# State space heads of one block: channels on partitions, heads in pairs, a channel mean by a matmul

## What is computed

```python
a_cum = jnp.cumsum(dt * A, axis=-1)
lmat = jnp.exp(segsum(a))
y_diag = jnp.einsum('bgcls,bgrcls,bcsgrp->bclgrp', cb, lmat, xc)
y_off = jnp.einsum('bclgn,bcgrpn,bgrcl->bclgrp', cc, prev_states, jnp.exp(a_cum))
y = y_f + flip(y_b) + d_skip[:, :, None] * xs
gated = y.reshape(bsz, length, g, r * p) * jax.nn.silu(zs)
gated = gated * lax.rsqrt(jnp.mean(gated * gated, axis=-1, keepdims=True) + EPS)
out = gated.reshape(bsz, length, D_SSD) * norm_w
```

## Time and profile before

| | us |
|---|---|
| median of 3 runs | 2029.85 (2029.8 to 2035.62) |
| profiled execution | 2027.07 |
| its span | 2025.3 |
| TensorE busy | 1749.7 (86%) |
| VectorE busy | 639.7 (32%) |
| ScalarE busy | 320.4 (16%) |
| GpSimd busy | 99.8 (5%) |
| transfers, mean over the span | 266 GB/s |

### The profile page before, as it was taken

How to read it: one execution, slowest core, us unless ns; L and a number is a source line. 1 busy time by engine, 2 the same in 40 slices (tenths; PEclk the granted TensorE clock), 3 DMA queues, 4 the chain that set the end, 5 groups by cost and what they waited for, 6 DMA issues and landing times.

```text
span 2025.3 us, 23132 instructions
## 1 busy us (share of the span) xinstructions
PE 1749.7 (86%) x9670; PEld 869.3 (43%) x9670; DVE 639.7 (32%) x1486; ACT 320.4 (16%) x715; POOL 99.8 (5%) x95
## 2 busy tenths in 40 slices
PE   6999999889999998989999989889998856665655
PEld 3844544444444476433333323246474423332322
DVE  2157828751310285231321312131353101010101
ACT  2112222210301265010000000020341000000000
POOL 0000112250200000000000000000000000000000
PEclk9899999889999999999999999999999978788877
DMA  8241238674612202179999999951308999999996
GB/s 331 104 167 58 109 125 319 262 287 175 241 42 83 83 1 98 55 299 427 428 428 428 427 427 427 427 211 52 140 1 332 377 427 427 427 427 427 427 427 267
DMA packets 39099, 538.20 MB, mean 266 GB/s; under 512 B 4330, under 2 KB 4714, under 8 KB 6612
## 3 DMA queue, kind: packets, MB, share of 16 engines
q1 hardware_dynamic: 37860, 530.85, 63.4%
q0 software_dynamic: 1136, 5.88, 0.8%
HBM read 535.66 MB, written 1.05 MB: 265 GB/s over the span
## 4 chain that ended last, share of the span: by engine, by line
PE 52%; issue 29%; DMA 10%; DVE 4%; POOL 2%; ACT 1%; DVEq 1%; POOLq 1%; SPq 0%; ACTq 0%
PE bank L596 51%; DMA mem<-in_moe 8%; PE bank L606 2%; DMA mem<-in_w_ada 1%; DVE mem L1306 1%; DVEq L1303 1%; POOL mem L2284 0%; POOLq L2285 0%; POOL mem L2296 0%; POOL mem L2287 0%; DMA mem<-in_ada_w 0%; POOL mem L2278 0%; POOL mem L2245 0%; DVE mem L1768 0%; ACT mem L1977 0%
## 5 line engine op out<-in xcount | busy, mean ns | idle before, releaser
L596 PE MATMUL bank<-mem 128*32 128x256 f32 (+10 forms) x8934 | 1642.7, 499 | 251.6 <-DMA mem<-in_moe 163.0
L596 PEld LDWEIGHTS bank<-mem 128*32 128x32 f32 (+5 forms) x8934 | 786.2, 151 | 1063.5 <-issue 753.7
L1977 ACT ACTIVATE mem<-bank 128x512 f32<-128x512 f32 (+5 forms) x279 | 141.5, 513 | 1165.6 <-PE bank L596 839.6
L1768 DVE TENSOR_TENSOR mem<-mem,bank 128x512 f32<-128x512 f32 (+1 forms) x32 | 17.7, 554 | 495.4 <-PE bank L596 495.4
L1785 DVE TENSOR_TENSOR mem<-bank,mem 32x512 f32<-32x512 f32 (+1 forms) x128 | 70.9, 554 | 226.6 <-PE bank L596 225.3
L606 PE MATMUL bank<-mem 128*128 128x128 f32 x680 | 109.6, 289 | 15.5 <-DVE mem L1768 5.0
L606 PEld LDWEIGHTS bank<-mem 128*128 128x128 f32 x680 | 80.1, 149 | 69.3 <-issue 38.4
L1443 DVE SCALAR_TENSOR_TENSOR mem<-mem 128x256 f32<-128x256 f32 x160 | 82.1, 513 | 9.6
L2245 POOL TENSOR_TENSOR mem<-mem 128x1 f32<-128x1 f32 (+5 forms) x16 | 14.5, 909 | 988.9 <-DVE mem L1306 988.9
L1306 DVE TENSOR_SCALAR mem<-bank,mem 128x256 f32<-128x256 f32 (+2 forms) x136 | 52.8, 451 | 15.2 <-PE bank L596 11.0
L1571 DVE TENSOR_REDUCE mem<-bank 128x1 f32<-128x512 f32 (+1 forms) x32 | 17.6, 549 | 104.3 <-PE bank L596 104.3
(11 more groups left out here) (178 smaller groups left out, 546.1 us busy)
## 6 DMA issues: line engine op xcount, KB each, us to landing
mem<-in_moe SPq DMA_DIRECT2D x192, 2048.0 KB, 35.1
mem<-in_ada_w SPq DMA_DIRECT2D x24, 2048.0 KB, 8.0
mem<-in_w_in SPq DMA_DIRECT2D x10, 2048.0 KB, 7.8
mem<-in_w_ada SPq DMA_DIRECT2D x6, 2048.0 KB, 12.3
mem<-in_even_w_in SPq DMA_DIRECT2D x6, 2048.0 KB, 10.2
mem<-in_w_out SPq DMA_DIRECT2D x4, 2048.0 KB, 8.3
mem<-in_odd_w_in SPq DMA_DIRECT2D x3, 2048.0 KB, 19.9
mem<-in_even_w_out SPq DMA_DIRECT2D x2, 2048.0 KB, 7.5
```

The source lines that it names most:

```text
L596: return nc.tensor.matmul(o, lhsT, rhs, start=start, stop=stop, skip_group_check=True)
L1977: took(name, S.activation(o, i, func))
```

## The change

- The heads work with channels on partitions. `pair_y(m)` computes two heads into one bank, head 2m in columns 0 to 63 of the array and 2m+1 in 64 to 127: four matmuls of 256 tokens with `m_mat`, and four more in the same bank with the initial states (`h_init`) and `c_dec`, the C matrix times exp of the decay. `off` is gone.
- `head_rows` makes the decay rows by four transposes of a broadcast column of `cum_col`. `cumT` is gone.
- ScalarE writes exp of the rows (`row_exp`, 512 columns) and six pieces of 128 columns of `m_mat`, with log dt in the bias; VectorE's `mixing` is one product of 768 columns and two adds.
- GpSimd multiplies `c_dec` for each head (128x512).
- `pair_out` adds the skip and gates. ScalarE squares, `pair_sum` takes the mean over a group's 384 channels by matmuls with 1/384, which leaves it on all partitions for each of 256 tokens. `group_ms` adds EPS, GpSimd's `group_rstd` raises it to -0.5 (128x256), and `group_out` scales.
- `zs` is computed with channels on partitions: 12 tiles of 256 columns instead of 6 of 512. `gated_T` is gone.
- The four products of `xw` stand together, behind `ct15`.

```diff
...
+        c_dec = [r.take(2, SEQ) for _ in range(4)]
...
+        dec_arg = [r.take(512) for _ in range(2)]
+        m_mat = [r.take(768) for _ in range(4)]
...
+        row_exp = [r.take(2, SEQ) for _ in range(2)]
+        y_ms = [r.take(SEQ) for _ in range(2)]
...
-            t = B.open("cumT", "dve")
-            for d, tab in enumerate((tri_f, tri_b)):
-                for q in range(2):
-                    last = mm(t.ps[0:24, SEQ * d:SEQ * d + SEQ], a_dt[:, q, 24 * d:24 * d + 24], tab[:, q, :], q == 0, q == 1)
-            B.close(t, last)
...
-                for j in range(2):
-                    t = B.open(f"zs{i}{j}", "act")
-                    B.close(t, token_major(t.ps[:, :], w, j, 0, 512))
+                for m in range(4):
+                    t = B.open(f"zs{4 * i + m}", "act")
+                    B.close(t, feature_major(t, w, P * m, P, 0, SEQ))
...
-                t = B.open(f"bc{h}", "dve")
-                B.close(t, mm(t.ps[:, :], ident[:, h:h + 1].to_broadcast([P, P]), cumT.rearrange("p a b -> p (a b)"), True, True))
...
+                t = B.open(f"bc{h}", "act")
+                for d in range(2):
                     for q in range(2):
...
+                        last = tr(t.ps[:, SEQ * d + P * q:SEQ * d + P * q + P], cum_col[:, q, 24 * d + h:24 * d + h + 1].to_broadcast([P, P]))
+                B.close(t, last)
+            def pair_y(m):
+                t = B.open(f"y{m}", "dve")
+                pe.wait_ge(m_ready, 2 * m + 2)
+                for q in range(2):
+                    for i in range(2):
+                        mm(t.ps[64 * i:64 * i + 64, 0:SEQ], xs_tok[:, q, P * m + 64 * i:P * m + 64 * i + 64],
+                           m_mat[(2 * m + i) % 4][:, SEQ * q:SEQ * q + SEQ], q == 0, False)
+                pe.wait_ge(c_dec_done, 2 * m + 2)
+                for d in range(2):
+                    for i in range(2):
+                        last = mm(t.ps[64 * i:64 * i + 64, 0:SEQ], h_init[:, d, P * m + 64 * i:P * m + 64 * i + 64],
+                                  c_dec[(2 * m + i) % 4][:, d, :], False, d == 1)
+                B.close(t, last)
+            group_sum = {}
+            def pair_sum(m):
+                g = m // 3
+                if m % 3 == 0:
+                    group_sum[g] = B.open(f"ss{g}", "dve")
+                t = group_sum[g]
+                pe.wait_ge(ssd_sq, m + 1)
+                last = mm(t.ps[:, 0:SEQ], mean_w, y_sq[m % 2], m % 3 == 0, m % 3 == 2)
+                if m % 3 == 2:
+                    B.close(t, last)
+                else:
+                    last.then_inc(sq_used, 1)
...
             head_rows(0)
             head_rows(1)
             for h in range(HEADS):
+                if h in ADA_AT_HEAD:
+                    ada_rows(ADA_AT_HEAD[h])
                 if h + 2 < HEADS:
                     head_rows(h + 2)
-                if h in ADA_AT_HEAD:
-                    ada_rows(ADA_AT_HEAD[h])
-                    if h:
-                        ada_outs(ADA_AT_HEAD[h] - 1)
-                head_y(h)
+                if h in ADA_AT_HEAD and h:
+                    ada_outs(ADA_AT_HEAD[h] - 1)
+                if h % 2:
+                    pair_y(h // 2)
+                    if h // 2 >= 2:
+                        pair_sum(h // 2 - 2)
...
-            for m in range(9):
-                pe.wait_ge(gated_done, 2 * (m // 3 + 1))
-                gated_T(m)
+            pair_sum(10)
+            pair_sum(11)
...
-                    if i == 2:
-                        pe.wait_ge(gated_done, 8)
-                        for m in range(9, 12):
-                            gated_T(m)
                     w = use(f"w_out{i}")
                     for q in range(4):
                         kt = 4 * i + q
                         if kt >= 4:
-                            wait_took(pe, f"gT{kt - 4}")
+                            pe.wait_ge(gated_done, kt - 3)
...
+            def decay_args(h):
+                ps = arrive(dve, f"bc{h}")
+                if h >= 2:
+                    wait_took(dve, f"bc{h - 2}")
+                for d in range(2):
+                    for q in range(2):
+                        i = P * (2 * d + q)
+                        last = scaled(dec_arg[h % 2][:, i:i + P], ps[:, i:i + P], cum_col[:, q, 24 * d + h:24 * d + h + 1], 0.0, ALU.subtract, ALU.min)
+                last.then_inc(args_done, 1)
+            def mixing(h):
+                wait_took(dve, f"bc{h}")
+                m = m_mat[h % 4]
+                V.tensor_tensor(m, m, cb[:, h // HPG, :], ALU.mult)
+                settle()
                 for q in range(2):
...
+                    o = m[:, 384 * q:384 * q + P]
+                    last = V.tensor_tensor(o, o, m[:, 512 + P * q:512 + P * q + P], ALU.add)
+                last.then_inc(m_ready, 1)
...
+            def pair_out(m):
+                ps = arrive(dve, f"y{m}")
+                x = mixT[:, 4 + m, :]
+                took(f"y{m}", V.scalar_tensor_tensor(out=y_t[m % 2], in0=x, scalar=G("d_skip")[:, m:m + 1], in1=ps[:, 0:SEQ], op0=ALU.mult, op1=ALU.add))
                 settle()
...
+                V.tensor_tensor(x, y_t[m % 2], zs[:, m, :], ALU.mult).then_inc(ssd_z, 1)
+            def group_ms(g):
+                ps = arrive(dve, f"ss{g}")
+                took(f"ss{g}", V.tensor_scalar(y_ms[g % 2], ps[:, 0:SEQ], EPS, None, ALU.add))
...
+                dve.wait_ge(ssd_rstd, g + 1)
+                for m in range(3 * g, 3 * g + 3):
+                    x = mixT[:, 4 + m, :]
+                    V.scalar_tensor_tensor(out=x, in0=x, scalar=G("ssd_norm")[:, m:m + 1], in1=y_ms[g % 2], op0=ALU.mult, op1=ALU.mult).then_inc(gated_done, 1)
...
             for h in range(HEADS):
                 mixing(h)
+                if h and h % 2 == 0:
+                    pair_out(h // 2 - 1)
+                if h >= 10 and h % 6 == 4:
+                    group_ms((h - 10) // 6)
                 if h + 2 < HEADS:
                     decay_args(h + 2)
                 if h in ADA_AT_HEAD and h:
                     ada_outs(ADA_AT_HEAD[h] - 1)
...
+                if h >= 12 and h % 6 == 0:
+                    group_out((h - 12) // 6)
+            pair_out(11)
+            group_out(2)
             for k in range(ADA_LEFT, 26):
                 ada_rows(k)
                 ada_outs(k - 1)
+            group_ms(3)
             settle()
             for n in (2, 3, 4):
                 gains(n)
...
+            group_out(3)
+            ada_rows(26)
+            ada_outs(25)
...
+                act.wait_ge(args_done, h + 1)
+                if h >= 2:
+                    act.wait_ge(c_dec_done, h - 1)
+                S.activation(row_exp[h % 2].rearrange("p d l -> p (d l)"), ps[:, :], ACT.Exp).then_inc(row_exp_done, 1)
+                if h >= 4:
+                    act.wait_ge(mm_done, tiles[f"y{(h - 4) // 2}"].no)
+                e, col = m_mat[h % 4], lambda a, d, q: a[:, q, 24 * d + h:24 * d + h + 1]
+                if h == 0:
+                    act.wait_ge(off_bias_done, 1)
+                S.activation(e[:, 128:256], ps[:, 128:256], ACT.Exp, bias=col(off_bias, 0, 0))
+                S.activation(e[:, 256:384], ps[:, 256:384], ACT.Exp, bias=col(off_bias, 1, 1))
+                for i, (d, q) in enumerate(((0, 0), (0, 1), (1, 0), (1, 1))):
+                    to = (0, 384, 512, 640)[i]
+                    last = S.activation(e[:, to:to + P], dec_arg[h % 2][:, P * i:P * i + P], ACT.Exp, bias=col(log_dt, d, q))
+                took(f"bc{h}", last)
...
-            wait_took(pool, "four3")
             for d in range(2):
-                if d:
-                    pool.wait_ge(mm_done, tiles["zs21"].no)
...
+            def group_rstd(g):
+                wait_took(pool, f"ss{g}")
+                Q.tensor_tensor(y_ms[g % 2], y_ms[g % 2], neg_half[:, 0:1].to_broadcast([P, SEQ]), ALU.pow).then_inc(ssd_rstd, 1)
+            for h in range(HEADS):
+                pool.wait_ge(row_exp_done, h + 1)
+                if h >= 4:
+                    pool.wait_ge(mm_done, tiles[f"y{(h - 4) // 2}"].no)
+                Q.tensor_tensor(c_dec[h % 4], row_exp[h % 2], c_fm[:, h // HPG, :].unsqueeze(1).to_broadcast([P, 2, SEQ]), ALU.mult).then_inc(c_dec_done, 1)
+                if h >= 11 and h % 6 == 5:
+                    group_rstd((h - 11) // 6)
+            group_rstd(3)
...
```

190 lines of the change are left out of this document (54 added, 136 removed).

## The result

The changed kernel takes 2113.36 us in the median of 4 runs (2107.01 to 2116.98), the kernel before 2029.82 beside it. The ratio is 1.040 (95% interval 1.037 to 1.044): slower, and near the 2120 us of the forecast. The way there was another one, as the trace shows.

A forecast was written before the change was run, and what follows sets the result against it. It took TensorE to set the pace in heads with an adaLN slab, VectorE in the others. Profiled 2027.07 - 33 (gain) + 117.6 (root stalls) + 6 (clock) = 2117.7, median 2.8 above: 2120 us; own range 2106 to 2138, with rival 1 from 2088.

The forecast's parts named there:

- rival 1: The root on GpSimd doesn't hold VectorE, so the stalls cost 95.4 instead of 117.6 us: 2098 us, chance 0.30.
- The price of the root: GpSimd's power of 128x256 takes 40.5 us (39.8 to 43.1), four times, by a straight line through narrower widths.
- That the root holds VectorE: The root keeps VectorE from two-input steps in SBUF: 39.2 us lost per root, three times, 117.6; chance 0.55.
- the clock: TensorE's clock restarts after three idle stretches of 35 us and more, 2 us each: 6 us (0 to 12).
- The gain without the roots: Without the new root's cost the change saves a net 33 us, of which the head loop's stretch gives 31.8.
- the pair: Two heads in the new loop take 9.0 us, set by VectorE, with TensorE at 7.5.
- the first pair: The loop starts as in the kernel before, with the first y after 7.1 us.
- the end: At the loop's end, the last pair's products, two slabs and two sums take 8.7 us.
- the ring: Not in the prediction: TensorE's pair products, sum, slab, decay rows, then VectorE's arguments and odd head's mixing, then the next pair.
- The decay rows by transposes: In the head loop, 8 transposes per pair at 0.13 us take 1.05, where two matmuls of 512 columns took 2.
- column groups: A pair's 8 matmuls of 256 columns lie in two groups of 64 columns that run beside each other: 1.8 us.
- The root of group 3: The last root, beside w_out's first slabs, costs nothing: done at +42.3, needed at +44.3; without cover up to 40 us.

The follow-up runs named there:

- root_2col: The changed kernel with each group's root cut to 2 of its 256 columns, in the same place of GpSimd's queue; 2021.26 us, ratio 0.995 to the kernel before.
- root_on_act: The changed kernel with the root on ScalarE as exp(-0.5 ln x), GpSimd keeping only its products; 2013.8 us, ratio 0.993 to the kernel before.
- c_dec_on_dve: The root_on_act kernel with GpSimd's product of decay row and C moved to VectorE, behind the same head's mixing; 2007.5 us, ratio 0.989 to the kernel before.

## Why the prediction was right, and where it was not

The whole time fell into the range, and the sign was right. The number was luck all the same: two errors of some 22 us each, in opposite directions, made it better than its working. The time alone would even have picked the wrong mechanism, as 2113 lies in the forecast's own range (2106 to 2138) and outside that of rival 1 (2088 to 2110), which the trace shows to be the true one.

- **The price of the root** held. 40.5 us were drawn from widths of 1 to 12 columns; it is 41.13, and 20.73 at half the width. A straight line over a factor of 20 in width was the step that decided the sign, and it was sound. (The slope between the widths of 1 and 12 columns is 0.159 and gives 41.1; the prediction took 0.157, and its own sum is 40.6.)
- **That the root holds VectorE** (the forecast's mechanism, 0.55) was wrong: 768 columns take 0.94 us in the middle of a root. Rival 1 was the right one. The step that failed is the choice between two rows that disagreed: I took the product of 2.8 us in the earlier trace rows, as the nearer in length, over the root of 2 columns in the same group, which was the same operation. The operation decides, not the length: a product holds VectorE for as long as it runs, a power of 41 us not at all. Of the three losses rival 1 gave (31.3, 31.3, 32.8, sum 95.4), root_2col shows 27.4, 31.2, 33.1, sum 91.7. Over the whole loop it is 95.5, but that contains the clock, which stood beside the 95.4 with 6 of its own. The interval from pair 5 to pair 6 by rival 1 is 43.0 - 2.7 = 40.3, and it is 40.14, but both ends were 4 us off: pair 5 starts 6.9 us behind the start of the root, since VectorE waits for decay rows first, and pair 6 at 47.1, since it waits for three held scalings and a mixing and not for two products.
- **The gain without the roots**, 33 us, was far too large. The loop of root_2col is 8.3 us shorter than that of the kernel before, where 31.8 stood. The failed terms: the pair (9.0 predicted, 10.6 measured, 17.7 us over eleven), the first pair (7.1 taken over from before; it is 11.48: 4.4, as the first products now stand behind two heads with their slabs and mixings and not one), the end (8.7; 10.02: 1.3). The sum is 23.4. TensorE's own 7.5 a pair was short too: it is 9.2 or 9.9 with two slabs and 6.4 with one, some 8 in the mean, as a column step with two matmuls of 512 columns takes 1.81 us where 0.92 stood for each step.
- **Why 9.0 was wrong.** Both sums, TensorE's 7.5 and VectorE's 9.0, were means over pairs, and the larger was taken as the pace. But the pairs alternate: with two slabs TensorE needs 9.2 to 9.9 by itself (11.2 and 11.7 where its clock fell, in root_on_act), with one it needs 6.4 and waits for the ring, 10.1 in the mean in root_on_act. The mean of the larger of two is more than the larger of two means. And GpSimd's hold, 2.0 a pair and of the right size in all (21.7 us or 1.8 a pair in root_on_act: 101.4 us busy, against 96.1 - 16.4 in c_dec_on_dve), was counted as work of an engine when it was time on the ring; taking it off the ring was worth 10.2 us of the loop, restarts of the clock included.
- **The decay rows by transposes** cost 0.49 per head (0.53 predicted), and the **column groups** overlap: 16 records of 256 columns in 1.88 us, against the 1.8 predicted. The transposes alone brought 2.6 us of the loop before instead of 10, since TensorE's saved time turned into waiting; the column groups weren't tried alone.
- **ScalarE** writes 1280 columns a head (512 and six times 128), not 1152. Its busy time in the loop went from 36.0 us to 69.7, twice as much, as forecast.
- **The root of group 3** costs nothing, and GpSimd's clears have 6.27 us to spare, against about 5 predicted. Both right.
- **The clock**: 6 us (0 to 12) for three restarts. After the three stalls TensorE runs at 0.50 for 4.9, 5.6 and 7.3 us more, at most half of it lost, 9 us; but root_2col has restarts of its own (23.9 us at 0.50 in its loop). The term is of the right size; how much of the 95.5 is clock, no run separates.
- **The sum**: forecast -33 + 117.6 + 6 = 90.6. Measured: -11.6 (loop -8.3, the stretches ahead and behind -3.3, which is less than the start of the loop moves between runs) + 95.5 = 83.9.

## What to carry to other kernels

Price an operation on an engine from rows of the same operation, and its side effects too: one root of 0.7 us beside VectorE said more about a root of 41 us than any product did. Don't take the larger of two averaged sums for the pace of a loop whose rounds alternate: follow one round of each kind from queue to queue, and ask for each step behind whom it stands. Keep what holds another engine off that ring, and count the holds into the price: VectorE took over 16.4 us of products, was busy for 5.3 us less, and the loop got 9.8 us shorter.

## What the runs showed of the hardware

- GpSimd's power costs 0.159 us a column from 1 to 256 columns, and holds up none of VectorE's two-input steps, with a constant or a streamed exponent (768 columns in 0.94 and 0.95 us beside it).
- GpSimd's products and VectorE's two-input steps hold each other, each for its own length: two adds of 0.49 us take 0.75 beside products of 256 columns with a constant column, 0.87 with a streamed operand, 1.40 beside one of 512, and a GpSimd product of 0.73 takes 1.27 when it starts in VectorE's step.
- GpSimd's own products of 256 columns are slower with a second streamed operand, 0.73 us against 0.61.
- Ln and exp in turn on ScalarE cost a table load of 1.28 us each time, two a root. Seven of the eight fall into the loop of root_on_act, and it is still 3.4 us shorter than that of root_2col.
